# Tile 1's expert search moves behind the first step, 40 V rows are fetched there alone, and the dot products read the activations from PSUM

## What is computed

```python
def peer_ffn(h, wq, subkeys, u, v):
    def block(hx):                                    # 128 tokens
        q = (hx @ wq).reshape(tb, 8, 2, 64)
        s1 = einsum('thd,nd->thn', q[:, :, 0], subkeys[0]); s2 = ... q[:, :, 1], subkeys[1]
        v1, i1 = top_k(s1, 16); v2, i2 = top_k(s2, 16)
        cand = v1[..., :, None] + v2[..., None, :]    # 256 candidates of each of 8 heads
        top, pos = top_k(cand, 16); eid = ...         # 8 x 16 = 128 experts of each token
        gate = softmax(top, axis=-1)
        act = gelu(einsum('td,thkd->thk', hx, u[eid]))          # 128 dot products of a token
        return einsum('thk,thkd->td', gate * act, v[eid])       # 128 weighted rows of a token
```

## Time and profile before

| | us |
|---|---|
| median of 3 runs | 5195.19 |
| lowest, highest | 5189.25, 5196.8 |
| span of the profiled execution, first to last instruction | 4964.1 |
| median less the profiled span | 231.1 |
| POOL busy in the span | 2886.0 (58%) |
| DVE busy in the span | 2756.6 (56%) |
| PE busy in the span | 2525.7 (51%) |
| first and last U gather issued, layer 1 and layer 2 | 847.5 to 2842.5, 3558.2 to 4762.5 |

### The profile page before, as it was taken

How to read it: one execution, slowest core, us unless ns; L and a number is a source line. 1 busy time by engine, 2 the same in 40 slices (tenths; PEclk the granted TensorE clock), 3 DMA queues, 4 the chain that set the end, 5 groups by cost and what they waited for, 6 DMA issues and landing times. The chain is left out here.

```text
span 4964.1 us, 36843 instructions
## 1 busy us (share of the span) xinstructions
PE 2525.7 (51%) x12033; PEld 1214.7 (24%) x12033; DVE 2756.6 (56%) x6177; ACT 524.5 (11%) x1108; POOL 2886.0 (58%) x2676
## 2 busy tenths in 40 slices
PE   7986888603434333343346775688611333333344
PEld 3435655500001000010014532365510000000001
DVE  2138558986656666566443400664897666745420
ACT  1017441000000000000000000453000000000000
POOL 1003201887777777777776773130287777777776
PEclk9988899856666666666677998889855666666578
DMA  6610021999999999999999998002289999999999
GB/s 203 189 38 27 2 101 59 326 342 393 406 404 395 408 408 392 408 407 393 407 385 340 402 401 325 26 20 92 103 317 351 390 409 408 394 409 409 408 394 364
DMA packets 472538, 1496.04 MB, mean 301 GB/s; under 512 B 59506, under 2 KB 116550, under 8 KB 468766
## 3 DMA queue, kind: packets, MB, share of 16 engines
q0 software_dynamic: 368640, 1342.34, 69.5%
q1 hardware_dynamic: 71112, 101.97, 6.1%
q10 hardware_dynamic: 32598, 49.39, 2.9%
...
## 5 line engine op out<-in xcount | busy, mean ns | idle before, releaser
L2031 DVE CUSTOM_DVE_ANT_0 experts_U<-experts_U,Y 128x1024 f32<-128x1024 f32 x1280 | 1563.0, 1223 | 1138.8 <-DMA experts_U<-in_peer_u_dram,experts_expert 1135.7
L1531 POOL DMA_INDIRECT experts_U<-in_peer_u_dram,experts_expert x1280 | 1392.9, 1088 | 899.1 <-DVE experts_expert L1357 489.9
L1873 PE MATMUL experts_acc<-experts_V,experts_lent 128*32 128x512 f32 x4608 | 938.5, 957 | 1573.6 <-DMA experts_V<-in_peer_v_dram,experts_turned 1572.3
L1548 POOL DMA_INDIRECT experts_V<-in_peer_v_dram,experts_turned x1152 | 1196.9, 1039 | 402.3 <-issue 341.9
L1873 PEld LDWEIGHTS experts_acc<-experts_V,experts_lent 128*32 128x32 f32 x4608 | 187.6, 150 | 2232.9 <-issue 2230.1
L427 PE MATMUL proj_acc<-W,HT 128*128 128x512 f32 (+2 forms) x832 | 319.0, 542 | 4.0 <-DMA W<-in_w_in_dram 2.5
L1979 DVE TENSOR_TENSOR experts_lent<-experts_acc,experts_G 128x1024 f32<-128x1024 f32 x10 | 12.2, 1221 | 350.9 <-PE experts_acc L1873 350.9
L427 PEld LDWEIGHTS proj_acc<-W,HT 128*128 128x128 f32 x832 | 156.7, 190 | 165.5 <-issue 138.3
L1830 PE MATMUL experts_keys<-experts_QT,Y 128*128 128x240 f32 (+1 forms) x832 | 183.8, 380 | 13.6 <-DMA experts_QT<-in_w_in_dram 12.5
L512 DVE COPY PR<-proj_acc 128x512 f32<-128x512 f32 (+2 forms) x52 | 32.3, 624 | 276.8 <-PE proj_acc L427 276.8
L1271 PE MATMUL experts_keys<-experts_sub,experts_QT 64*128 64x128 f32 x320 | 40.6, 391 | 281.1 <-DVE experts_rest L1289 279.6
...
## 6 DMA issues: line engine op xcount, KB each, us to landing
...
experts_U<-in_peer_u_dram,experts_expert POOLq DMA_INDIRECT x1280, 6.6
...
```

Source lines behind the costliest of these rows:

```text
L1531: pool.indirect_dma_start(s.U[:, n % RING], None, u_rows, bass.IndirectOffsetOnAxis(ap=s.expert[:, j % 2, k:k + 1], axis=0)).then_inc(ug[n ...
L1548: pool.indirect_dma_start(into, None, v_rows, bass.IndirectOffsetOnAxis(ap=s.turned[:, i % 2, e:e + 1], axis=0)).then_inc(done, 16)
L1873: mm = nc.tensor.matmul(acc[32 * c:32 * c + 32, i % 2, half], s.spread[:, e * 32:e * 32 + 32], v_slot(V * GROUP + c)[0][:, 512 * half:512 ...
L2031: nc.vector.tensor_tensor_reduce(out=s.U[:, n % RING], in0=s.U[:, n % RING], in1=s.H[:, tiles[j]], scale=1.0, scalar=0.0, op0=ALU.mult, op ...
```

## The change

Five things are different; the number of gathers, dot products, search pieces and matmuls stays.

1. In step 0 the search of tile 1 is advanced only at every sixth dot product from the ninth on (20 of its 85 pieces). Six more come right after the last dot product, then the weights of tile 0, then all that is left, in one run.
2. Between the U gathers of tile 0 and those of tile 1, POOL issues V gathers 8 to 39 of tile 0 alone. They go through both rings, since no U gather is under way.
3. In step 1 the V gathers run ahead of where they ran: V gather 40 follows the fifth U gather, tile 0's last V gather follows U gather 92, and tile 1's first eight come from place 96 on. Step 1 has 128 U and 96 V gathers, step 2 has 128 and 112, later steps 128 and 128 as before.
4. Before the dot products of a tile, ACT copies its activations (128x1024) into two banks of PSUM (`hold_h`), and the dot products read them there: all of tiles 0 and 1, and from the 41st on for later tiles. The last tile of the first layer reads SBUF as before.
5. PE's loop is written out by steps to match. Key scores of heads 0 to 3 of tile 1 come in step 0, of heads 4 and 5 before the first V group, of heads 6 and 7 before the fourth.

```diff
+    OUT_AT, TURNED_AT, HELD_AT = 28, 48, 40
+    HELD_STEPS = T - 1 if more else T
+    AHEAD_AT = {0: [76 + 4 * n for n in range(RING)], 1: [96 + 4 * n for n in range(RING)]}
+    LEAD, LAG = RING // 2, RING
+    ALONE = 5 * RING
+    SIDE_STEP, HELD = 6, 6
+    SCORES_AT = {0: 0, 20: 1}
...
+        def h_bank(j):
+            return acc[:, 1 if j < 2 else j % 2].rearrange("p a b -> p (a b)")
...
 # GpSimd
+                def ask_u(j, k):
+                    n = j * SLOTS + k
+                    if k in (0, SLOTS // 2):
+                        pool.wait_ge(sems.chosen, 2 * j + 1 + 2 * k // SLOTS)
+                    if SLOTS <= n < SLOTS + RING:
+                        pool.wait_ge(sums, (ALONE - 2 * RING + k) // GROUP + 1)
+                    elif n >= RING:
+                        pool.wait_ge(dots, n - RING + 1)
...
+                def ask_v(v):
...
+                        if RING <= v < 2 * RING:
+                            pool.wait_ge(dots, SLOTS - RING + v % RING + GROUP)
...
+                        elif 2 * RING <= v < ALONE or v >= TAIL + 2 * RING:
+                            pool.wait_ge(sums, v // GROUP - 2 * RGROUPS + 1)
...
+                for j in range(T):
+                    for k in range(SLOTS):
+                        ask_u(j, k)
+                        if j == 1 and LEAD <= k < SLOTS + LEAD - ALONE:
+                            ask_v(ALONE + k - LEAD)
+                        elif j < 2 and k in AHEAD_AT[j]:
+                            ask_v(j * SLOTS + AHEAD_AT[j].index(k))
+                        elif j >= 2 and (j - 1) * SLOTS + k - LAG >= SLOTS + RING:
+                            ask_v((j - 1) * SLOTS + k - LAG)
+                    if j == 0:
+                        for v in range(RING, ALONE):
+                            ask_v(v)
 # ScalarE
+                def hold_h(j):
+                    nc.scalar.activation(h_bank(j), s.H[:, tiles[j]], ACT.Copy).then_inc(held_h, 1)
...
                         act.wait_ge(dots, SLOTS * j)
+                        if j == 1:
+                            hold_h(1)
...
+                        if 2 <= j < HELD_STEPS:
+                            act.wait_ge(scaled, j - 1)
+                            hold_h(j)
...
-                    if j + 1 < T:
+                    if j == 1:
+                        softmax_exp(nc, act, s, sems, 1)
+                    if 0 < j < T - 1:
                         softmax_exp(nc, act, s, sems, j + 1)
 # TensorE
+                for g in range(GROUPS):
+                    beside(0, g)
+                turn_weights(1)
+                ahead, behind = ALONE // GROUP, LAG // GROUP
+                for g in range(GROUPS + ahead):
+                    if g in (0, 3):
+                        scores(1, 2 + g // 3)
+                    if g >= ahead:
+                        beside(1, g - ahead)
+                    if g < GROUPS:
+                        weighted_sum(0, g)
+                for j in range(2, T + 1):
+                    for g in range(GROUPS if j < T else GROUPS + behind):
...
 # VectorE
-                        nc.vector.tensor_tensor_reduce(out=s.U[:, n % RING], in0=s.U[:, n % RING], in1=s.H[:, tiles[j]],
+                        if j < HELD_STEPS and k == (0 if j < 2 else HELD_AT):
+                            dve.wait_ge(held_h, j + 1)
+                        h = h_bank(j) if j < 2 or HELD_AT <= k and j < HELD_STEPS else s.H[:, tiles[j]]
+                        nc.vector.tensor_tensor_reduce(out=s.U[:, n % RING], in0=s.U[:, n % RING], in1=h,
...
-                        if j and k == WEIGHTS_AT:
+                        if j >= 2 and k == WEIGHTS_AT:
                             weigh(j - 1)
...
-                        elif k >= SIDE_AT:
+                        elif k >= SIDE_AT and (j or (k - SIDE_AT) % SIDE_STEP == 0):
                             next(finding, None)
...
+                    if j == 0:
+                        for _ in range(HELD):
+                            next(finding, None)
+                        weigh(0)
+                        for _ in finding:
+                            pass
```

159 lines of the change are left out of this document (84 added, 75 removed).

## The result

| | median us | runs | ratio of the two, 95% interval |
|---|---|---|---|
| before | 5194.7 | 4 (5189.3 to 5196.8) | |
| after | 5148.4 | 4 (5147.9 to 5154.4) | 0.991 [0.9898, 0.9922] |

The changed kernel is faster, by 46 us where 100 were forecast. The profiled execution of it took 5147.86 us with a span of 5146.1, a difference of 1.8 us. That alone is news: the profile of before, with its span of 4964.1 us, stands 231 us under the runs it was shown with, and such a difference lies in no other run of this study.

The account below looks back on a forecast made before the run. POOL's gathers were taken as the bound, held by dot products in step 0 and paced by DMA in full steps. Layer sums of -53 and -49 us took 5195 to 5093, given as 5095, range 5075 to 5150.

Parts of the forecast that it names:

- Do the holds go: Open step: POOL's gathers in step 0, held during dot products, drop from 1.32 to 0.94 us with the PSUM operand.
- no release: Rival: the PSUM operand does not free POOL's held gathers; +46 us together, 5140 us; chance 0.12.
- half pace: Rival: dot products from PSUM take 2.44 us, not 1.22, so DVE bounds step 0; +339 us, 5534; chance 0.06.
- Step 0: Stretch of tile 0's dot products: 187 us in the first layer, 182 in the second, -38 and -35.
- three limits: Step 0's bounds once the holds are gone: POOL 169 us, DVE 159, DMA 175.
- PE has no late place in it: Between tiles 0 and 1, the last key scores come in time, wanted at 17 us after the last dot product.
- later: Steps after step 2: first layer two steps at 339 us, -4 each; second layer as before.
- The stretch alone: From tile 0's last dot product to tile 1's first, with V gathers only: +45 us in each layer.
- What the 32 gathers give back: Steps 1 and 2 have 16 gathers fewer each: -28 and -24 us first layer, -34 and -25 second.
- rests on fewer held gathers: Condition for steps 1 and 2 to reach 1.285 us a gather: fewer gathers held by dot products.
- The search in a run is late: Rival: tile 1's search delays its U gathers, POOL idling some 22 us a layer; 5139 us; chance 0.11.
- 358 GB/s: HBM-to-SBUF rate set aside: a gather would cost 1.46 us, step 0 at least 199, some 15 us more a layer.

Follow-up runs that it names:

- e5: The changed kernel again, unaltered, on chip C: 4857.74 us, 0.9794 of the kernel before.
- e12: The changed kernel with all dot products reading activations from SBUF instead of PSUM, on chip D: 4923.05 us, 0.9906 of the kernel before.
- C: A batch of runs on one chip, of the quicker kind; the kernel before took 4964.2 us there.
- e2: The changed kernel with tile 0's expert numbers turned right after the first key scores in step 0, on chip B: 5134.0 us, 0.9924 of the kernel before.
- e1: The kernel before, unchanged, run again on chip B: 5171.13 us, ratio 1.000.
- D: A batch of runs on one chip, of the quicker kind; the kernel before took 4969.9 us there.
- B: A batch of runs on one chip, of the slower kind; the kernel before took 5171.5 us there.
- e8: The changed kernel with queries two tiles at a time, 40 search pieces and the third key scores kept in step 0, on chip C: 4862.79 us, 0.9799.
- A: The batch of the main result, on one chip of the slower kind; the kernel before took 5194.7 us there.
- e4: The kernel before with only the dot products' activations moved to PSUM, old order kept, on chip B: 5125.62 us, 0.9905 of the kernel before.
- e3: The changed kernel with all dot products reading activations from SBUF instead of PSUM, on chip B: 5138.7 us, 0.9929 of the kernel before.
- e13: The kernel before with added, unused 1 MB memory-to-memory copies, on a slower-kind chip: 5319.66 us, 1.0222 of the kernel before.
- e14: The changed kernel with added, unused 1 MB memory-to-memory copies, on a slower-kind chip: 5225.1 us, 1.0045 of the kernel before.
- the wide one: The changed kernel with queries of tiles 2 to 5 computed two tiles at a time: 4866.41 us on C, 4867.1 on D, 5133.25 (0.987) on a slower-kind chip.
- e17: The changed kernel with at most six U rows asked for and unused in step 0, on a slower-kind chip: 5153.84 us, 0.9902 of the kernel before.

## Why the prediction came out as it did

**The durations belonged to another kind of chip than the median.** I noted 231 us between profile and runs, and left them. Where before takes 4964 to 4970 us, as in the profile, the change brings -106 us twice, against -102 summed. Layer by layer, e5 minus: -51 (forecast -53) and -44 (forecast -49). That the first comes so near is partly luck: its step 2 gave 6 us less than forecast, and its last step, forecast as before, 14 us more (402.2 to 388.6), which nothing here explains. The number that was asked for was that of a chip where gathers take 1.42 us, and there the same sum doesn't hold.

**Do the holds go: right.** POOL's gathers take 0.94 us in step 0, the fused row costs 1.22, and the rivals "no release" and "half pace" fall. The rule of the Trainium skill (SBUF — State Buffer, Who interferes with whom), that one SBUF input does not contend, agrees with e5's row of 0.94 beside the PSUM dot product. With both inputs in SBUF e12's gather is held, 1.99 us.

**Step 0: right in its three limits, and its first-layer value is the step that failed.** 182 and 187 came out at 176 and 185 on C. On the slower kind the second layer's has 190 to 195: 136 x 1.42 = 193 by the DMA, so here the pace matters. The first layer's, forecast at 187, took 232. The prediction had three limits there, POOL, DVE and DMA. It lacked a fourth, TensorE, for which the vector engine waited 41.8 us there: in the profile I read it was late with nothing, and I read no row of its gaps because there were none. I wrote "PE has no late place in it" of the stretch alone, and did not put the question for step 0.

Same chip, e2 minus e1 against the forecast, in us:

| | step 0 | alone | step 1 | step 2 | later | sum |
|---|---|---|---|---|---|---|
| first layer | +11.0 (-38) | +52.3 (+45) | -29.3 (-28) | -23.6 (-24) | -17.8 (-8) | -7.4 (-53) |
| second layer | -25.4 (-35) | +53.3 (+45) | -34.3 (-34) | -19.8 (-25) | -2.9 (0) | -29.1 (-49) |

65 us are missing, and 49 of them are the first layer's step 0. The second layer's step 0 and the two stretches alone lack 10 and 16 us more, and the later steps give 9 back.

**The stretch alone: 45 against 48.5 and 52 to 56.** On C POOL takes 40.1 us from the last dot product (1034.2) to the first U gather of tile 1, not 37.5, and the first dot product comes 8.4 us after that, not 7.5. On the slower kind the key scores of the last two heads come late, and with them the expert numbers that POOL waits for, in after by these rows. The matmuls of these scores end at 1102.4 in the trace, and why the vector engine goes on only 9 us later stays open; TensorE itself starts on its slow beat there (1108.87, 1110.28 and 1111.69 us). So "PE has no late place in it" held on C and D and failed on the slower kind.

```profile
1111.80 0.50 DVE L1283 MAX8 experts_val<-experts_keys 128x8 f32<-128x128 f32 x2 [6.83 <-remote]
...
1132.91 1.67 POOL L1553 DMA_INDIRECT experts_U<-in_peer_u_dram,experts_expert  x1 [5.20 <-DVE experts_expert L1357]
```

**What the 32 gathers give back: right in step 1** (-27 and -34 on C, -29 and -34 on B, forecast -28 and -34), and 5 to 7 us short in step 2 in three of four cases (-18.5 and -18.0 on C, -19.8 in B's second layer, forecast -24 and -25; only B's first layer has its -23.6). That step 1 reaches its pace "rests on fewer held gathers" was wrong: e12 has the holds and needs 302.7 and 287.7 us, as e5 does.

**The rivals.** "The search in a run is late" named 5139, close to the 5148, and mostly by luck: on C the stretch doesn't wait for the search (e8), and on A POOL waits 5.2 us for it, through late key scores, where the rival had 22. The Trainium skill's 358 GB/s (same page, Summary: rules for kernel authors), which I set aside for the 409 of the rows, is near the 362 to 381 of the slower kind and far from C's 397 to 409. No one number holds for all the chips here.

**What stays open.** Shown is that TensorE's instructions start late, each at its own price, on a fixed beat, and that the vector engine and POOL wait for it: 42 us in after, 24 with half the instructions. Late starts as such come with the slower kind and not with the change, since e1 has them. What the change brings is a long stretch of them where step 0 can't bear it. Counting, in the first layer's step 0, matmuls that start 0.65 to 2.95 us after the one before with idle time that ends in "issue", and in groups of four or more: 35 in after between 864 and 927 us, 4 in e4 between 872 and 875, none in e1, e3, e13 and e14. So the long stretch was seen with the new order and PSUM dot products together and without filler copies, one profile of each kernel. What brings it about isn't shown, nor whether the slower kind is the chip's or comes from something beside the kernel, such as another core at work on the same memory; the "unknown queue" on all its pages leaves both open. The kernel before and after on one chip in two batches would tell.

**The version to keep** is the wide one: equal to the changed kernel on the quicker kind, and on the slower kind at 0.987 where the changed kernel, there and in e17, has 0.990 to 0.991. It was compared across chips of that kind, each with the kernel before beside it, not on one. On that kind the PSUM operand alone, in the old order, has 0.9905 (e4), as much as the whole change.
